# Finishing a stage's two output banks one behind the other, and reading them bank by bank, in a two-block transformer kernel

## The chip, the cores and the metric

The kernel runs on one core of one Trainium2 chip. The metric is the device time of one execution in microseconds (us).

## The reference

`reference()` runs two blocks on 256 tokens of width 1024, all in float32. The first block is a short-convolution mixer and a SwiGLU feed-forward (width 2816), both under adaptive modulation, and a final norm. The second has two layers; each is feed-forward, mixer (a 31-tap convolution with sliding-window attention, or a forgetting attention), feed-forward. What matters here is how a stage ends. In the first block it is `x = x + g * y`; in the second the stage's output `y` is itself normed before it is added:

```
def _rmsnorm(x, g):
    xf = x.astype(jnp.float32)
    y = xf * lax.rsqrt(jnp.mean(xf * xf, axis=-1, keepdims=True) + EPS)
    return (y * g.astype(jnp.float32)).astype(x.dtype)
...
    h = _swiglu(_rmsnorm(x, g[0]), ...)
    x = x + 0.5 * _rmsnorm(h, g[1])
    h = _rmsnorm(x, g[2])
    h = _mixer_even(h, ...)
    x = x + _rmsnorm(h, g[3])
```

## The kernel before

**Eight stages in a row.** CONV, FFN0 (first block), FFN1, AB, FFN2, FFN3, FOX, FFN4 (second block), numbered 0 to 7; `b` is the stage that ends and `s = b + 1` the one that begins. The order of the work on each engine is written out by hand, and semaphores are the only thing that ties the engines together. Tokens are two tiles of 128 (`t` = 0, 1). A weight arrives by DMA (SP's queue) as a unit of 128x2048, is split into a high part by ScalarE (`w_hi`, L995, L1000, L1012) and a low part by VectorE (`w_lo`, L1372, L1377, L1394, L1396), and TensorE forms each product from three matmuls (`product`, L512 to L514).

**How a stage ends.** The output of token tile `t` stands in the two PSUM banks `4+2t` and `5+2t`, 512 columns each. The stage's last weight unit is applied by `down_part` (L557), first for tile 0 and then for tile 1: for each of two contraction slices `k` and each bank `h` one product, so 12 matmuls a tile, and the banks alternate. `y_tok0` counts the end of tile 0 and `w_used` that of tile 1. A few matmuls on a matrix of ones (`keep_warm`, L539) follow.

**What then runs between two stages** (`between`). For the stages of the second block, ScalarE squares all 1024 columns out of PSUM and sums them (`root_y`, L1017, with a read of the accumulator behind it), and takes the root with `eps` as bias (L1019); VectorE takes the reciprocal (L1402), scales the output by it and by a row into `tmp` (`residual`, L1423, 1024 columns), and adds it to `x` in two halves (L1428, 512 columns each, counted by `x_new`). For CONV and FFN0 there is no root of y: VectorE multiplies by a row (L1418) once tile and row are there.

**Order on the engines there.** `s` is NORMED (FFN0, AB, FOX) if its input is normed before it is transposed: VectorE does residual 0, `norm_x` 0 (L1442), residual 1, `turned_lo` 0 (L1453: the low part of the transposed x), `norm_x` 1, `turned_lo` 1. It is FOLDED (FFN1 to FFN4) if x itself is transposed and the norm is folded into later steps: residual 0, `turned_lo` 0, residual 1, `turned_lo` 1. TensorE transposes a tile in two halves of four (`turn_x`, L532; in a FOLDED stage each half waits for its half of x), runs 8 `keep_warm` matmuls, waits for the first `xT_lo` and starts with the first half of tile 0. ScalarE's order in a FOLDED stage is root_y 0, `turned_hi` 0 (L1034), root_y 1, root_x 0, a weight split, `turned_hi` 1; in a NORMED one root_y 0, root_x 0, root_y 1, `turned_hi` 0 and so on. Ahead of all this ScalarE splits the unit `BASE[s] + 1` in four pieces (`split_late`, L1012), and VectorE takes three of these ahead of residual 0 and the fourth behind it.

## Time and profile before

| | us |
|---|---|
| median of 3 runs | 1398.92 |
| lowest and highest run | 1398.75, 1401.97 |
| the profiled execution, its own time | 1401.05 |
| its span, first to last instruction | 1399.3 |
| TensorE (matmuls) busy | 1315.8 (94%) |
| VectorE busy | 831.5 (59%) |
| ScalarE busy | 670.7 (48%) |
| GpSimd busy | 156.8 (11%) |
| DMA queue of the weights, share of 16 engines | 52.9% |

The span is divided into 40 slices on the page, and TensorE is busy nine tenths or more in most of them. Matmuls overlap, so their busy time is above the rate at which they start: 128x512 matmuls last 0.39 us each and start about 0.227 us apart.

### The profile page before, as it was taken

The page shows a single profiled execution, that of the slowest core. Times are in us where ns is not written, and L with a number is a line of the kernel's source. Part 1 is how long each engine was busy: PE and PEld are TensorE (multiplying, and loading weights), DVE is VectorE, ACT ScalarE, POOL GpSimd, SP SyncE. Part 2 cuts the span into 40 slices and gives each one's busy share as a digit, 9 for nine tenths or more (in the row PEclk, how much of TensorE's full clock was granted, in tenths as well). Part 3 has the DMA queues.
Part 4 walks back from the last instruction along what each step waited for, and adds up shares of the span by engine and source line. Part 5 has one row for each costly group of instructions (what it writes and reads, how often), then busy time and mean ns, then how long its engine had stood idle before and what let it go on. Part 6 is the DMA issues. An engine that isn't in the chain of part 4 may idle for free.

```text
span 1399.3 us, 18491 instructions
## 1 busy us (share of the span) xinstructions
PE 1315.8 (94%) x6809; PEld 1101.6 (79%) x6809; DVE 831.5 (59%) x1017; ACT 670.7 (48%) x992; POOL 156.8 (11%) x121
## 2 busy tenths in 40 slices
PE   1869899999899999888999999999999999999998
PEld 1869688888788888776788888888888888788886
DVE  5998665444665555644655556655555477555554
ACT  2304343444554445544654456545544465655443
POOL 1880392000500000200000000000000100000000
PEclk9979999999999999999999999999999999999999
DMA  9967575555355556460375555555572433265551
GB/s 335 343 231 254 181 240 180 182 191 196 106 183 192 194 188 203 142 175 31 122 237 183 180 195 181 180 181 180 184 236 90 150 136 119 93 227 193 180 195 61
DMA packets 171581, 253.64 MB, mean 181 GB/s; under 512 B 9785, under 2 KB 135949, under 8 KB 171533
## 3 DMA queue, kind: packets, MB, share of 16 engines
q1 hardware_dynamic: 168352, 244.33, 52.9%
q0 software_dynamic: 2304, 8.41, 1.6%
q8 instruction: 33, 0.54, 0.2%
q10 hardware_dynamic: 878, 0.25, 0.1%
q14 instruction: 14, 0.11, 0.0%
HBM read 249.77 MB, written 1.05 MB: 179 GB/s over the span
## 4 chain that ended last, share of the span: by engine, by line
PE 84%; DVE 9%; ACT 3%; DMA 1%; issue 1%; POOL 0%; DVEq 0%; SPq 0%; ACTq 0%; POOLq 0%
PE ps L512 26%; PE ps L514 25%; PE ps L513 25%; DVE tmp L1575 2%; PE ps L554 2%; DVE w_lo L1372 2%; DVE x_sb L1428 1%; DMA raw<-in_ada_w 1%; PE ps L813 1%; PE ps L532 1%; DVE tmp L1423 1%; DVE tmp L1525 1%; PE ps L698 1%; ACT w_hi L1012 1%; ACT tmp L1017 0%
## 5 line engine op out<-in xcount | busy, mean ns | idle before, releaser
L512 PE MATMUL ps<-w_lo,xT_hi 128*128 128x512 f32 (+1 forms) x960 | 382.2, 398 | 4.8 <-DVE xT_lo L1453 2.7
L1372 DVE TENSOR_TENSOR w_lo<-raw,w_hi 128x2048 fp32r<-128x2048 f32 x117 | 278.1, 2379 | 166.3 <-ACT w_hi L995 166.3
L514 PE MATMUL ps<-w_hi,xT_lo 128*128 128x512 f32 (+1 forms) x960 | 374.4, 390 | 0.0
L513 PE MATMUL ps<-w_hi,xT_hi 128*128 128x512 f32 (+1 forms) x960 | 374.0, 390 | 0.0
L1377 DVE SCALAR_TENSOR_TENSOR w_lo<-raw,par,w_hi 128x512 fp32r<-128x512 f32 x336 | 230.4, 748 | 139.7 <-ACT w_hi L1000 139.5
L995 ACT ACTIVATE w_hi<-raw 128x2048 fp32r<-128x2048 f32 x117 | 223.5, 1912 | 181.8 <-PE ps L514 160.0
L512 PEld LDWEIGHTS ps<-w_lo,xT_hi 128*128 128x128 f32 x960 | 182.1, 190 | 41.9 <-DVE xT_lo L1453 3.0
L1000 ACT ACTIVATE w_hi<-raw,par 128x512 fp32r<-128x512 f32 x336 | 214.3, 712 | 0.8 <-PE ps L514 0.8
L514 PEld LDWEIGHTS ps<-w_hi,xT_lo 128*128 128x128 f32 x960 | 181.4, 189 | 38.5
L513 PEld LDWEIGHTS ps<-w_hi,xT_hi 128*128 128x128 f32 x960 | 182.2, 190 | 35.6 <-issue 0.2
L512 PE MATMUL ps<-w_lo,hT_hi 128*128 128x512 f32 x400 | 156.5, 391 | 0.0
L514 PE MATMUL ps<-w_hi,hT_lo 128*128 128x512 f32 x400 | 155.7, 389 | 0.0
L513 PE MATMUL ps<-w_hi,hT_hi 128*128 128x512 f32 x400 | 155.6, 389 | 0.0
L512 PE MATMUL ps<-xT_lo,w_hi 128*128 128x256 f32 x360 | 108.7, 302 | 15.9 <-DVE w_lo L1372 13.8
L1092 ACT ACTIVATE hT_hi<-ps 128x512 fp32r<-128x512 f32 x50 | 29.9, 599 | 185.7 <-PE ps L554 185.7
L513 PE MATMUL ps<-xT_hi,w_hi 128*128 128x256 f32 x360 | 105.9, 294 | 0.0
L514 PE MATMUL ps<-xT_hi,w_lo 128*128 128x256 f32 x360 | 105.6, 293 | 0.0
L1499 DVE TENSOR_TENSOR hT_lo<-ps,hT_hi 128x512 fp32r<-128x512 f32 x50 | 34.5, 691 | 103.0 <-ACT hT_hi L1092 103.0
L1087 ACT ACTIVATE act_pair<-ps,stat 128x256 f32<-128x256 f32 x88 | 41.2, 468 | 103.1 <-PE ps L514 103.0
L512 PEld LDWEIGHTS ps<-xT_lo,w_hi 128*128 128x128 f32 x360 | 73.2, 203 | 21.4 <-DVE w_lo L1372 11.2
L513 PEld LDWEIGHTS ps<-w_hi,hT_hi 128*128 128x128 f32 x400 | 75.1, 188 | 15.7 <-issue 0.2
L514 PEld LDWEIGHTS ps<-w_hi,hT_lo 128*128 128x128 f32 x400 | 75.1, 188 | 15.7
(224 smaller groups left out, 1443.5 us busy)
## 6 DMA issues: line engine op xcount, KB each, us to landing
raw<-in_ffn_w_gate SPq DMA_DIRECT2D x88, 512.0 KB, 4.0
raw<-in_ffn_w_up SPq DMA_DIRECT2D x88, 512.0 KB, 4.9
raw<-in_ffn_w_down SPq DMA_DIRECT2D x88, 512.0 KB, 4.1
raw<-in_ffn_w_in SPq DMA_DIRECT2D x44, 512.0 KB, 4.7
raw<-in_conv_w_in SPq DMA_DIRECT2D x24, 512.0 KB, 5.4
raw<-in_fox_w_in SPq DMA_DIRECT2D x24, 512.0 KB, 4.3
raw<-in_ffn_w_out SPq DMA_DIRECT2D x22, 512.0 KB, 4.4
raw<-in_ada_w SPq DMA_DIRECT2D x16, 512.0 KB, 6.5
```

The costliest lines, as they stand in the source:

```text
L512: pe.matmul(o, a_hi, b_lo, start=first, stop=False, skip_group_check=True)
L513: pe.matmul(o, a_hi, b_hi, start=False, stop=False, skip_group_check=True)
L514: return pe.matmul(o, a_lo, b_hi, start=False, stop=last, skip_group_check=True)
L554: tr = pe.transpose(ps[:, 2, f * SEQ + t * P:f * SEQ + (t + 1) * P], hid[:, t, tok(f)], ident[:, :])
L995: act.activation(w_hi[:, slot_of(n), :], raw[:, slot_of(n), :], ACT.Copy).then_inc(hi_ready, 1)
L1000: a = act.activation(w_hi[:, slot_of(n), c], raw[:, slot_of(n), c], ACT.Copy, scale=par[:, g + k:g + k + 1])
L1087: act.activation(sil[:, t, :], ps[:, t, 0:FCH], ACT.Silu, scale=stat[:, 2, c:c + 1] if s in FOLDED else 1.0).then_inc(sil_done, 1)
L1092: act.activation(dst, ps[:, 2, :].rearrange("p (f c) -> p f c", f=2), ACT.Copy).then_inc(hT_hi_ok, 1)
L1372: dve.tensor_tensor(w_lo[:, slot_of(n), :], raw[:, slot_of(n), :], w_hi[:, slot_of(n), :].bitcast(F32), ALU.subtract).then_inc(raw_done, 1)
L1377: o = dve.scalar_tensor_tensor(w_lo[:, slot_of(n), c], raw[:, slot_of(n), c], par[:, g + k:g + k + 1], w_hi[:, slot_of(n), c].bitcast(F32) ...
L1499: dve.tensor_tensor(dst, ps[:, 2, :].rearrange("p (f c) -> p f c", f=2), hi.bitcast(F32), ALU.subtract).then_inc(hT_ok, 1)
L1575: o = dve.scalar_tensor_tensor(acc, ada_v_raw[:, q % 2, i, :], cond[:, k:k + 1], acc, ALU.mult, ALU.add)
```

## The change

The last unit of a stage goes through a new function, `tail_part`, which does both slices of bank `4+2t` and then both of bank `5+2t`, and counts a new semaphore `y_half` after the first bank; the number and the kind of matmuls stay. `root_y` squares and sums each bank by itself, adds `eps` to the first sum with a small activation of its own, and takes the root of the second sum with the first as bias. `residual` does scale, add, scale, add, each on 512 columns, where it did one scale on 1024 and two adds.

```diff
--- before.py
+++ after.py
@@ -283,6 +283,8 @@
         y_tok0 = sem("y_tok0")
         y_sq = sem("y_sq")
         y_std = sem("y_std")
+        y_half = sem("y_half")
+        y_eps = sem("y_eps")
         y_rstd = sem("y_rstd")
         x_sq = sem("x_sq")
         x_std = sem("x_std")
@@ -564,6 +566,18 @@
                                      hi[:, c], lo[:, c], first and k == 0, last and k == 1)
                 return mm
 
+            def tail_part(n, aT_hi, aT_lo, k0, t, ks=(0, 1)):
+
+                hi, lo = unit(n)
+                for h in range(2):
+                    for k in ks:
+                        c = slice(k * D + h * 512, k * D + (h + 1) * 512)
+                        mm = product(ps[:, 4 + 2 * t + h, :], aT_hi[:, k0 + k, tok(t)], aT_lo[:, k0 + k, tok(t)],
+                                     hi[:, c], lo[:, c], False, k == 1)
+                    if h == 0:
+                        mm.then_inc(y_half, 1)
+                return mm
+
             def ffn(s):
                 f, n = ffn_index(s), BASE[s]
                 turn_x(s, 0)
@@ -621,8 +635,8 @@
                 down_part(last - 1, hT_hi, hT_lo, 0, 0, False, False, ks=(1,))
                 down_part(last - 1, hT_hi, hT_lo, 0, 1, False, False).then_inc(w_used, 1)
                 pe.wait_ge(hT_ok, NCH * (f + 1))
-                down_part(last, yT_hi, yT_lo, 0, 0, False, True).then_inc(y_tok0, 1)
-                down_part(last, yT_hi, yT_lo, 0, 1, False, True).then_inc(w_used, 1)
+                tail_part(last, yT_hi, yT_lo, 0, 0).then_inc(y_tok0, 1)
+                tail_part(last, yT_hi, yT_lo, 0, 1).then_inc(w_used, 1)
                 if s != FFN4:
                     keep_warm(WARM_FOLDED if s + 1 in FOLDED and s > FFN0 else WARM_FINAL if s == FFN0 else WARM_NORMED)
 
@@ -754,10 +768,12 @@
             for i in range(4):
                 pe.wait_ge(yT_ok, i // 2 + 1)
                 first, last = i == 0, i == 3
-                mm = down_part(n + 12 + i, yT_hi, yT_lo, 2 * i, 0, first, last)
                 if last:
-                    mm.then_inc(y_tok0, 1)
-                down_part(n + 12 + i, yT_hi, yT_lo, 2 * i, 1, first, last).then_inc(w_used, 1)
+                    tail_part(n + 12 + i, yT_hi, yT_lo, 2 * i, 0).then_inc(y_tok0, 1)
+                    tail_part(n + 12 + i, yT_hi, yT_lo, 2 * i, 1).then_inc(w_used, 1)
+                else:
+                    down_part(n + 12 + i, yT_hi, yT_lo, 2 * i, 0, first, False)
+                    down_part(n + 12 + i, yT_hi, yT_lo, 2 * i, 1, first, False).then_inc(w_used, 1)
                 if i == 2:
                     pe.wait_ge(ada_p_done, ADA_CH)
                     row_everywhere(2, ada_acc)
@@ -864,8 +880,8 @@
             pe.wait_ge(yT_ok, 3)
             down_part(n + 9, yT_hi, yT_lo, 0, 0, False, False)
             down_part(n + 9, yT_hi, yT_lo, 0, 1, False, False).then_inc(w_used, 1)
-            down_part(n + 10, yT_hi, yT_lo, 2, 0, False, True).then_inc(y_tok0, 1)
-            down_part(n + 10, yT_hi, yT_lo, 2, 1, False, True).then_inc(w_used, 1)
+            tail_part(n + 10, yT_hi, yT_lo, 2, 0).then_inc(y_tok0, 1)
+            tail_part(n + 10, yT_hi, yT_lo, 2, 1).then_inc(w_used, 1)
             ffn(FFN2)
             ffn(FFN3)
             n = BASE[FOX]
@@ -944,7 +960,10 @@
 
             def out_part(u, t):
                 pe.wait_ge(oT_ok, 4 + 2 * (u - 12) + 2)
-                mm = down_part(n + u, yT_hi, yT_lo, 2 * (u - 12), t, u == 12, u == 15)
+                if u == 15:
+                    mm = tail_part(n + u, yT_hi, yT_lo, 2 * (u - 12), t)
+                else:
+                    mm = down_part(n + u, yT_hi, yT_lo, 2 * (u - 12), t, u == 12, False)
                 if t == 1:
                     mm.then_inc(w_used, 1)
                 elif u == 15:
@@ -1019,10 +1038,18 @@
                 act.activation(stat[:, 1, c:c + 1], stat[:, 0, c:c + 1], ACT.Sqrt, bias=eps[:, 0:1]).then_inc(std, 1)
 
             def root_y(b, t):
+                e = 2 * (b - FFN1) + t
+                first, second, std = stat[:, 0, STAT_Y + e:STAT_Y + e + 1], stat[:, 2, STAT_Y + e:STAT_Y + e + 1], \
+                    stat[:, 1, STAT_Y + e:STAT_Y + e + 1]
+                act.wait_ge(y_half, 2 * b + t + 1)
+                act.activation(xn[:, t, 0:512], ps[:, 4 + 2 * t, :], ACT.Square, scale=D ** -0.5, accum_out=first).then_inc(y_sq, 1)
+                act.wait_ge(y_sq, 2 * e + 1)
+                act.activation(first, first, ACT.Identity, bias=eps[:, 0:1]).then_inc(y_eps, 1)
                 act.wait_ge(w_used if t else y_tok0, weight_count(y_unit(b)) if t else b + 1)
-                e = 2 * (b - FFN1) + t
-                square_root(STAT_Y + e, ps[:, 4 + 2 * t:6 + 2 * t, :].rearrange("p b n -> p (b n)"), xn[:, t, :],
-                            y_sq, y_std, e + 1)
+                act.activation(xn[:, t, 512:D], ps[:, 5 + 2 * t, :], ACT.Square, scale=D ** -0.5, accum_out=second).then_inc(y_sq, 1)
+                act.wait_ge(y_sq, 2 * e + 2)
+                act.wait_ge(y_eps, e + 1)
+                act.activation(std, second, ACT.Sqrt, bias=first).then_inc(y_std, 1)
 
             def root_x(e, t):
 
@@ -1406,25 +1433,26 @@
             def rms_x(e, t):
                 return reciprocal_root(2 * e + t, x_std, x_rstd, 2 * e + t + 1)
 
-            def output(t):
-                return ps[:, 4 + 2 * t:6 + 2 * t, :].rearrange("p b n -> p (b n)")
-
             def residual(b, t):
 
                 if b == FFN0:
                     dve.wait_ge(ada_row_a, 4)
-                if b <= FFN0:
-                    dve.wait_ge(w_used if t else y_tok0, weight_count(y_unit(b)) if t else b + 1)
-                    dve.tensor_tensor(tmp[:, t, :], output(t), rows[:, 2 if b else 1, :], ALU.mult).then_inc(t_done, 1)
-                    scale = 1.0
-                else:
-                    e = 2 * (b - FFN1) + t
-                    r = reciprocal_root(STAT_Y + e, y_std, y_rstd, e + 1)
-                    dve.scalar_tensor_tensor(tmp[:, t, :], output(t), r, rows[:, 1, :], ALU.mult, ALU.mult).then_inc(t_done, 1)
-                    scale = 1.0 if b in (AB, FOX) else 0.5
-                dve.wait_ge(t_done, 2 * b + t + 1)
+                e = STAT_Y + 2 * (b - FFN1) + t
+                r = reciprocal_root(e, y_std, y_rstd, e - STAT_Y + 1) if b > FFN0 else None
+                scale = 1.0 if b in (CONV, FFN0, AB, FOX) else 0.5
                 for h in range(2):
                     c = slice(h * 512, (h + 1) * 512)
+                    y = ps[:, 4 + 2 * t + h, :]
+                    if b <= FFN0:
+                        if h == 0:
+                            dve.wait_ge(y_half, 2 * b + t + 1)
+                        else:
+                            dve.wait_ge(w_used if t else y_tok0, weight_count(y_unit(b)) if t else b + 1)
+                        o = dve.tensor_tensor(tmp[:, t, c], y, rows[:, 2 if b else 1, c], ALU.mult)
+                    else:
+                        o = dve.scalar_tensor_tensor(tmp[:, t, c], y, r, rows[:, 1, c], ALU.mult, ALU.mult)
+                    o.then_inc(t_done, 1)
+                    dve.wait_ge(t_done, 4 * b + 2 * t + h + 1)
                     o = dve.scalar_tensor_tensor(x[:, t, c], tmp[:, t, c], scale, x[:, t, c], ALU.mult, ALU.add)
                     if b != FFN0:
                         o.then_inc(x_new, 1)
```

**ScalarE from the end of FFN1 into AB** (xn is a scratch output, `stat` a column of sums and roots). Before:

```order
L1017 ACTIVATE xn,stat<-ps 128x1024 [waits y_tok0]
L1019 ACTIVATE stat<-stat,eps 128x1 [waits y_sq]
L1017 ACTIVATE tmp,stat<-x_sb 128x1024 [waits x_new]
L1019 ACTIVATE stat<-stat,eps 128x1 [waits x_sq]
L1017 ACTIVATE xn,stat<-ps 128x1024 [waits w_used]
L1019 ACTIVATE stat<-stat,eps 128x1 [waits y_sq]
```

With the change:

```order
L1045 ACTIVATE xn,stat<-ps 128x512 [waits y_half]
L1047 ACTIVATE stat<-stat,eps 128x1 [waits y_sq]
L1049 ACTIVATE xn,stat<-ps 128x512 [waits y_tok0]
L1052 ACTIVATE stat<-stat 128x1 [waits y_eps,y_sq]
L1036 ACTIVATE tmp,stat<-x_sb 128x1024 [waits x_new]
L1038 ACTIVATE stat<-stat,eps 128x1 [waits x_sq]
L1045 ACTIVATE xn,stat<-ps 128x512 [waits y_half]
L1047 ACTIVATE stat<-stat,eps 128x1 [waits y_sq]
L1049 ACTIVATE xn,stat<-ps 128x512 [waits w_used]
L1052 ACTIVATE stat<-stat 128x1 [waits y_eps,y_sq]
```

Each `root_y` was two activations and is four now; two of the four wait for sums of the engine itself, and both of its squares stand in front of what follows on ScalarE.

**VectorE in the same place, from `norm_x` of tile 0 to `turned_lo` of tile 0.** Before:

```order
L1442 SCALAR_TENSOR_TENSOR xn<-x_sb,stat,rows 128x1024 [waits x_rstd]
L1402 RECIPROCAL stat<-stat 128x1 [waits y_std]
L1423 SCALAR_TENSOR_TENSOR tmp<-ps,stat,rows 128x1024 [waits y_rstd]
L1428 SCALAR_TENSOR_TENSOR x_sb<-tmp,x_sb 128x512 [waits t_done]
L1428 SCALAR_TENSOR_TENSOR x_sb<-tmp,x_sb 128x512
L1453 TENSOR_TENSOR xT_lo<-ps,xT_hi 128x4x128 [waits xT_hi_ok] x2
```

With the change:

```order
L1470 SCALAR_TENSOR_TENSOR xn<-x_sb,stat,rows 128x1024 [waits x_rstd]
L1429 RECIPROCAL stat<-stat 128x1 [waits y_std]
L1453 SCALAR_TENSOR_TENSOR tmp<-ps,stat,rows 128x512 [waits y_rstd]
L1456 SCALAR_TENSOR_TENSOR x_sb<-tmp,x_sb 128x512 [waits t_done]
L1453 SCALAR_TENSOR_TENSOR tmp<-ps,stat,rows 128x512
L1456 SCALAR_TENSOR_TENSOR x_sb<-tmp,x_sb 128x512 [waits t_done]
L1481 TENSOR_TENSOR xT_lo<-ps,xT_hi 128x4x128 [waits xT_hi_ok] x2
```

One instruction on 1024 columns has become two on 512, and the second stands between the two adds; `turned_lo`, for which TensorE waits, is behind all four.

## Rows read from the trace of the kernel before

**Rows 1.** The page: the chain that ended last, share of the span by engine
```profile
PE 84%; DVE 9%; ACT 3%; DMA 1%; issue 1%; POOL 0%; DVEq 0%; SPq 0%; ACTq 0%; POOLq 0%
```
**Rows 2.** Groups by shape: line, engine, out<-in, shape, count | busy us, mean ns
```profile
L1017 ACT ACTIVATE xn<-ps 128x1024 f32<-128x1024 f32 x12 | 12.2, 1018 | 8.5 <-PE ps L514 8.4
L1034 ACT ACTIVATE xT_hi<-ps 128x512 fp32r<-128x512 f32 x28 | 15.7, 592 | 22.0 <-PE ps L532 21.8
L1423 DVE SCALAR_TENSOR_TENSOR tmp<-ps,stat,rows 128x1024 f32<-128x1024 f32 x12 | 15.4, 1284 | 0.4
L1492 DVE SCALAR_TENSOR_TENSOR act_pair<-ps,stat,act_pair 128x256 f32<-128x256 f32 x88 | 39.1, 477 | 16.5 <-ACT act_pair L1087 16.5
L1418 DVE TENSOR_TENSOR tmp<-ps,rows 128x1024 f32<-128x1024 f32 x4 | 4.9, 1214 | 0.0
L1453 DVE TENSOR_TENSOR xT_lo<-ps,xT_hi 128x512 fp32r<-128x512 f32 x28 | 18.2, 685 | 12.6 <-ACT xT_hi L1034 12.1
```
**Rows 3.** Timeline, end of FFN4: start us, us, engine, what [idle before <-releaser]
```profile
1389.72 1.03 ACT L1017 ACTIVATE xn<-ps 128x1024 f32<-128x1024 f32 x1 [6.18 <-PE ps L514]
1390.87 0.29 ACT L1019 ACTIVATE stat<-stat,eps 128x1 f32<-128x1 f32 x1
1391.46 1.28 DVE L1423 SCALAR_TENSOR_TENSOR tmp<-ps,stat,rows 128x1024 f32<-128x1024 f32 x1
1392.78 1.29 DVE L1428 SCALAR_TENSOR_TENSOR x_sb<-tmp,x_sb 128x512 f32<-128x512 f32 x2
```
**Rows 4.** Timeline, CONV to FFN0
```profile
157.03 1.89 DVE L1394 TENSOR_TENSOR w_lo<-raw,w_hi 128x512 fp32r<-128x512 f32 x3 [3.26 <-ACT rows L1185]
158.84 1.22 DVE L1418 TENSOR_TENSOR tmp<-ps,rows 128x1024 f32<-128x1024 f32 x1
174.06 1.09 PE L532 MATMUL ps<-ident,xn 128*128 128x128 f32 x8 [1.95 <-DVE xn L1446]
```
**Rows 5.** Timeline, FFN1 to AB
```profile
552.52 2.20 ACT L1012 ACTIVATE w_hi<-raw 128x512 fp32r<-128x512 f32 x4 [1.68 <-PE ps L514]
555.18 1.03 ACT L1017 ACTIVATE xn<-ps 128x1024 f32<-128x1024 f32 x1 [0.46 <-PE ps L514]
562.01 0.29 ACT L1019 ACTIVATE stat<-stat,eps 128x1 f32<-128x1 f32 x1
562.41 0.16 DVE L1402 RECIPROCAL stat<-stat 128x1 f32<-128x1 f32 x1
565.87 0.50 PE L512 MATMUL ps<-w_lo,xT_hi 128*128 128x512 f32 x1 [1.33 <-DVE xT_lo L1453]
```
**Rows 6.** Timeline, AB to FFN2 (granted clock low at its start)
```profile
671.77 1.28 ACT L983 ACT_TABLE_LOAD   x1
676.90 1.26 PE L532 MATMUL ps<-ident,x_sb 128*128 128x128 f32 x8 [2.37 <-DVE x_sb L1428]
677.99 1.87 PE L539 MATMUL ps<-ones 128*128 128x128 f32 x8
679.51 0.77 PE L512 MATMUL ps<-w_lo,xT_hi 128*128 128x512 f32 x1
681.67 1.29 DVE L1428 SCALAR_TENSOR_TENSOR x_sb<-tmp,x_sb 128x512 f32<-128x512 f32 x2
683.01 1.02 PEld L532 LDWEIGHTS ps<-ident,x_sb 128*128 128x128 f32 x8
```
**Rows 7.** Timeline, FFN2 to FFN3
```profile
863.93 1.03 ACT L1017 ACTIVATE xn<-ps 128x1024 f32<-128x1024 f32 x1
868.76 1.06 PE L539 MATMUL ps<-ones 128*128 128x128 f32 x8
869.74 0.50 PE L512 MATMUL ps<-w_lo,xT_hi 128*128 128x512 f32 x1
872.38 0.39 PE L514 MATMUL ps<-w_hi,xT_lo 128*128 128x512 f32 x1
873.79 0.42 PEld L532 LDWEIGHTS ps<-ident,x_sb 128*128 128x128 f32 x4 [0.18 <-DVE x_sb L1428]
```

## The prediction

> **What bounds the kernel now.** I first read the chain that ended last: 84% of it is TensorE and 12% VectorE and ScalarE [rows 1]. Within a stage TensorE runs without a break, so an edit here is worth something only where TensorE waits, which is between two stages. So I read the timeline of each of the eight stage ends, the idle time ahead of TensorE's instructions above all. Three patterns are to be seen.
>
> First, when a stage ends, VectorE and ScalarE are mostly late for a reason of their own, not because the second bank is missing. Ahead of residual 0 VectorE is still on the weight pieces in CONV, where the scaling starts as they end [rows 4], and FFN0 looks the same. In FFN1 ScalarE's four pieces end at 554.72, and its square of tile 0 starts at 555.18 after only 0.46 us of idle [rows 5]; FFN3 repeats this. In AB a table load ends at 673.05 [rows 6], while tile 0 is complete at about 671.8 (TensorE's work ends 2.37 us ahead of 676.90, and tile 1's twelve matmuls take 2.72 of the time before), and FOX repeats it; in FFN2 the square starts with no idle time before it [rows 7]. Only FFN4 has ScalarE waiting for a long time, 6.18 us [rows 3].
>
> Second, TensorE's restart hangs on whole halves that come late in the order. In a FOLDED stage the second four transposes wait for the second half of x (0.18 us idle in [rows 7]), and the first matmul stands behind them and 8 warming matmuls. In a NORMED one the first matmul waits 1.33 us for `xT_lo`, which stands behind the whole residual of tile 1 [rows 5].
>
> Third, for tile 1 both banks have been complete for microseconds when ScalarE gets to it, so nothing of that tile can start earlier by being read bank by bank.
>
> **What each part costs.** The reordered 12 matmuls cost nothing: same shapes, and runs of twelve on one bank already start 0.227 us apart elsewhere (the first twelve of FFN3 take 2.64 us from first start to last [rows 7], a step of 0.24). Bank one is complete 6 x 0.227 = 1.36 us earlier than bank two; that is all that can be gained on a tile.
>
> *ScalarE's root.* Before: square at 1389.72, root at 1390.87, so 1.15 us [rows 3]. A square of one bank is not shown; the nearest rows are 1018 ns for 1024 columns and 592 ns for 512 [rows 2], so halving takes off 0.42 and square to dependent step is 0.73. The small activation that adds eps is like the root, after which the next instruction can start 0.20 later. With both banks there, root_y takes 0.73 + 0.20 + 0.73 = 1.66 to the root, 0.52 more than before (bounds: 0, if the eps step and the second sum hide behind the first square; 0.61, if the next square starts only when the small one's 0.29 are over). Where bank two is what it waits for, the root comes 0.41 earlier.
>
> *VectorE's residual.* Before: scale 1.284, dependent add 1.32 after its start [rows 3], second add 0.60 after the first, 0.69 long: 2.61. A 512-column scale out of PSUM lies between 477 ns for 256 and 1284 ns for 1024 [rows 2]; the straight line gives 0.746. So 0.79 + 0.60 + 0.79 + 0.69 = 2.87, that is 0.26 more; the first half of x is there after 1.48 instead of 2.01, the second 0.26 later. For CONV and FFN0 it is 1214 against 685 ns [rows 2], 0.19 more a tile. Bounds of the 0.26: 0.05 if a half costs half of 1.284 (0.64), and 0.68 if it costs twice the 477 ns for 256 columns; the line lies between, as VectorE's 685 and 1214 ns do. The Trainium skill (Perfetto Trace Analysis, Optimizing Scalar/DVE Operations) gives a fixed overhead of about 125 ns for a VectorE operation on PSUM and 51 ns for a ScalarE one; with these in place of 0.26 and (with 93 ns for the small one) 0.52, the sum below would be an estimated 2 us, not 6.4. The rows decide, since they hold the semaphore round trips too.
>
> *Stage by stage, in delay of TensorE's stream:*
> - CONV and FFN0: both residuals are on the chain, 2 x 0.19 each: 0.38 + 0.38. The earlier first bank gives nothing, since VectorE is on the weight pieces until then [rows 4].
> - FFN1 and FFN3: the first square can start at 554.62 but the second only after it, so root 0 comes at 556.28 instead of 556.33; x is 0.21 later. Root 1 is queued behind it on ScalarE and 0.52 longer, ready at 562.01 + 0.29 + 0.73 = 563.03, while VectorE was free for it at 562.41 [rows 5]: 0.66. Residual 1 adds 0.26, and `turned_lo` and TensorE's first matmul come 0.92 later: 0.92 + 0.92.
> - AB and FOX: root 0 is 0.52 later, the first half of x comes at the same time, the second 0.78 later, and so do the second transposes, the warming matmuls and the first product [rows 6]. For tile 1 root and scale are 1.30 later and the second half of x 1.56. That half was there at 682.96, and its transposes, the fifth of eight loads from 683.01 on, at about 683.50 [rows 6]; with one 1.56 later and the other 0.78, TensorE waits 0.28 more in AB, and 0.40 in FOX by the same rows there: 1.06 + 1.18.
> - FFN2: ScalarE can take the first square up to 0.2 us earlier, so root 0 is 0.42 late and the second half of x 0.68. For tile 1 there is no slack (TensorE waits for x already, rows 7): another 0.52 + 0.26. Total 1.46.
> - FFN4: root 0 is 0.41 earlier, but the reciprocal of tile 1 then waits for VectorE, which has 0.26 more to do twice: about 0.1 later.
>
> Queued behind the waiting instructions: on ScalarE the weight split of the next stage and `turned_hi` 1, on VectorE the fourth weight piece; both move with the same delay, and their readers on TensorE are as late. SP's weight loads wait for VectorE's low parts and have 47% of the queue's time free. The sum is 0.76 + 1.84 + 2.24 + 1.46 + 0.1 = 6.4 us. Within a stage TensorE has no idle time to absorb it. Against the profiled execution (1401.05, which is 2.1 over the median of the runs shown) this is 1407.5; against the median 1398.9 + 6.4 = 1405.3.
>
> **Rivals.**
> *A, the clock falls at more stage starts (chance 0.17).* After AB, where TensorE has been idle for 2.37 us, the 8 warming matmuls take 1.87 us, and of the twelve behind them the last starts 3.50 us after the first, with the first load of the transposes at 683.01; after FFN2, at full clock, it is 1.06 and 2.64 [rows 6, 7]. A fall costs 0.81 + 0.86 = 1.67 us. FFN1, FFN2 and FFN3 restart at full clock now; their waits grow from 1.33 to some 2.0 us (FFN1, FFN3) and by a new gap of 0.7 in FFN2. If all three fall: 1405.3 + 5.0 = 1410.3. Against it: the gaps stay under AB's.
> *B, ScalarE's additions are hidden (chance 0.17).* If the eps step and second sum cost nothing, only VectorE's part is left: 0.76 for CONV and FFN0, 0.52 each for FFN1 and FFN3, 0.26 each for AB and FOX, 0.5 for FFN2, 0.1: 2.9 us, 1401.8, within what can be told from nothing. For it: root_y's first part has 1.36 us under the second bank wherever ScalarE is free; against it: it is free only in FFN4, and never for tile 1.
> *C, it is faster (chance 0.05).* Mechanism: at tile 0 the root comes 0.41 earlier and the first half of x a further 0.53, and TensorE's transposes start on it. The Trainium skill has the rule for it in the same section as above: breaking up instructions of engines that are not saturated but cause bubbles elsewhere may let work finish sooner. Here it would need ScalarE free when bank one is done, at six stage ends: 6 x 0.94 = 5.6 us, 1393.3. It decides from the point where the square waits for matmuls by over 0.9 us, and only FFN4's does; also TensorE waits for the second half, which comes only 0.15 earlier then.
> *D, the change doesn't do what it says:* covered by the above, since wherever ScalarE is late the two halves are simply one after the other.
>
> **How the numbers follow.** Forecast 0.61, A 0.17, B 0.17, C 0.05. A measurement can tell about 0.3%, 4.2 us, from no change. The forecast of 6.4 us is slower in nearly all of its spread (0.58 of 0.61, with most of its own range from 4 to 9), A is slower (0.17), B the same: slower 0.75, same 0.20, faster 0.05. The range runs from 1401.0, which takes in B, to 1410.5, which takes in A.
>
> **What would show it.** Right: root_y 1 takes about 1.66 us from first square to root; the scales last about 0.75; TensorE's first product after FFN1 is idle for about 2 us before it; FFN2's gap between the two halves of transposes grows to 0.8 or so; TensorE's matmuls in the last unit start 0.227 apart as before. Wrong: if ScalarE's first square starts over 1 us before the second at most stage ends and TensorE's idle times shrink, C holds; if new stretches at 1.2 GHz appear behind FFN1, FFN2 or FFN3, A does.

## The result and the profile after

Nine runs of the changed kernel have a median of 1408.57 us (1403.0 to 1410.38), nine of the kernel before on the same chip 1401.04 (1398.75 to 1402.65). The ratio is 1.0050, 95% interval 1.0036 to 1.0064: **slower by 7.0 us (5.0 to 9.0)**, where 6.4 was forecast. Here and below a difference in us is this ratio's; the medians alone are 7.5 apart. A second series, five runs against nine, gave 1.0055 (1.0041 to 1.0069). The profiled execution took 1407.87 us, its span is 1406.1 (1399.3 before).

The chain of work that ended last, on the page of the changed kernel:

```profile
PE 82%; DVE 10%; ACT 4%; issue 2%; DMA 1%; POOL 0%; SPq 0%; DVEq 0%; ACTq 0%; POOLq 0%
```

TensorE's share fell from 84% [rows 1] by what VectorE and ScalarE gained. TensorE's work is the same (1316.1 us busy against 1315.8). The new instructions in the groups by line and shape (count | busy us, mean ns | idle time before and its releaser):

```profile
L1045 ACT ACTIVATE xn<-ps 128x512 f32<-128x512 f32 x12 | 7.0, 585 | 5.1 <-PE ps L516 5.1
L1047 ACT ACTIVATE stat<-stat,eps 128x1 f32<-128x1 f32 x12 | 3.5, 295 | 0.4
L1049 ACT ACTIVATE xn<-ps 128x512 f32<-128x512 f32 x12 | 7.0, 581 | 0.7 <-PE ps L516 0.7
L1453 DVE SCALAR_TENSOR_TENSOR tmp<-ps,stat,rows 128x512 f32<-128x512 f32 x24 | 17.9, 748 | 0.4
L1451 DVE TENSOR_TENSOR tmp<-ps,rows 128x512 f32<-128x512 f32 x8 | 5.4, 681 | 0.0
```

Both halves together last 1.17 us where the square was 1.018, and 1.50 where the scale was 1.284 [rows 2]. The idle column of the squares tells more: the twelve first squares wait 5.1 us in all, and all of it is FFN4's (4.79 for tile 0 and 0.34 for tile 1). At every other stage end the first bank was there before ScalarE was.

FFN1's end on ScalarE, tile 1 (start, duration, engine, line):

```profile
559.93 0.58 ACT L1045 ACTIVATE xn<-ps 128x512 f32<-128x512 f32 x1
...
560.63 0.29 ACT L1047 ACTIVATE stat<-stat,eps 128x1 f32<-128x1 f32 x1
560.83 0.58 ACT L1049 ACTIVATE xn<-ps 128x512 f32<-128x512 f32 x1
...
561.53 0.29 ACT L1052 ACTIVATE stat<-stat 128x1 f32<-128x1 f32 x1
```

From first square to root it is 1.60 us, one thing behind the other, 1.15 before [rows 3]. VectorE now waits for it, and then does the longer residual:

```profile
561.86 0.16 DVE L1429 RECIPROCAL stat<-stat 128x1 f32<-128x1 f32 x1 [0.32 <-ACT stat L1052]
562.05 0.75 DVE L1453 SCALAR_TENSOR_TENSOR tmp<-ps,stat,rows 128x512 f32<-128x512 f32 x1
562.84 0.69 DVE L1456 SCALAR_TENSOR_TENSOR x_sb<-tmp,x_sb 128x512 f32<-128x512 f32 x1
563.45 0.74 DVE L1453 SCALAR_TENSOR_TENSOR tmp<-ps,stat,rows 128x512 f32<-128x512 f32 x1
564.23 0.69 DVE L1456 SCALAR_TENSOR_TENSOR x_sb<-tmp,x_sb 128x512 f32<-128x512 f32 x1
564.84 1.28 DVE L1481 TENSOR_TENSOR xT_lo<-ps,xT_hi 128x512 fp32r<-128x512 f32 x2
```

And TensorE behind both, at the ends of FFN1 (one row), AB (two) and FFN2 (two, and the last one's weight loads):

```profile
565.58 0.50 PE L514 MATMUL ps<-w_lo,xT_hi 128*128 128x512 f32 x1 [1.99 <-DVE xT_lo L1481]
...
678.96 0.66 PE L534 MATMUL ps<-ident,x_sb 128*128 128x128 f32 x4 [2.31 <-DVE x_sb L1456]
680.35 1.12 PE L534 MATMUL ps<-ident,x_sb 128*128 128x128 f32 x4 [0.73 <-DVE x_sb L1456]
...
872.19 0.66 PE L534 MATMUL ps<-ident,x_sb 128*128 128x128 f32 x4 [0.62 <-DVE x_sb L1456]
...
878.44 0.66 PE L534 MATMUL ps<-ident,x_sb 128*128 128x128 f32 x4 [0.73 <-DVE x_sb L1456]
878.44 0.42 PEld L534 LDWEIGHTS ps<-ident,x_sb 128*128 128x128 f32 x4 [0.97 <-DVE x_sb L1456]
```

The wait for `xT_lo` was 1.33 us before [rows 5]; behind FFN2 the loads of the second half of tile 1's transposes waited 0.18 us [rows 7] and wait 0.97 now. The first half of x does let TensorE start, but TensorE then waits for the second.

Not waiting for the first bank doesn't mean that the early bank had no taker. At FFN1 ScalarE had waited 0.46 us for the second bank in before [rows 5]; now it starts at once, while TensorE is still on that bank. ScalarE's tile 0 and the stage's last matmul, changed and before:

```profile
553.52 0.58 ACT L1045 ACTIVATE xn<-ps 128x512 f32<-128x512 f32 x1
...
555.12 0.29 ACT L1052 ACTIVATE stat<-stat 128x1 f32<-128x1 f32 x1
...
556.37 0.39 PE L516 MATMUL ps<-w_hi,yT_lo 128*128 128x512 f32 x1
```

```profile
556.33 0.29 ACT L1019 ACTIVATE stat<-stat,eps 128x1 f32<-128x1 f32 x1
...
557.48 0.39 PE L514 MATMUL ps<-w_hi,yT_lo 128*128 128x512 f32 x1
```

Against the last matmul the first square is 0.55 us earlier than the one square was (2.85 us ahead of it, where it was 2.30), and the root 0.10 (1.25 ahead, where it was 1.15): the longer chain takes the rest. FFN3 is the same, and in FFN2 the first square is 0.19 earlier and the root 0.26 later.

FFN4 is the only place where ScalarE waits for the first bank:

```profile
1395.17 0.60 ACT L1045 ACTIVATE xn<-ps 128x512 f32<-128x512 f32 x1 [4.79 <-PE ps L516]
...
1396.53 0.60 ACT L1049 ACTIVATE xn<-ps 128x512 f32<-128x512 f32 x1 [0.34 <-PE ps L516]
...
1397.25 0.30 ACT L1052 ACTIVATE stat<-stat 128x1 f32<-128x1 f32 x1
```

From the second square to the root it is 0.72 us, so the root comes 0.43 earlier than with one square.

**One measure for all kernels.** To compare stage ends I took, from the starts of TensorE's rows in the timeline, the time from the last matmul of the ending stage to the thirteenth product matmul of the next (the first of tile 1). It holds all waits of the stage end. "Rest" is everything between these, and the tail is from FFN4's last matmul to the end. In us:

| kernel (profile) | CONV | FFN0 | FFN1 | AB | FFN2 | FFN3 | FOX | sum | tail | rest |
|---|---|---|---|---|---|---|---|---|---|---|
| before | 14.36 | 14.52 | 12.06 | 9.89 | 7.98 | 12.06 | 9.89 | 80.8 | 7.29 | 1311.3 |
| before, 2nd | 14.44 | 13.98 | 12.07 | 9.88 | 7.98 | 12.10 | 9.91 | 80.4 | 7.29 | 1312.5 |
| changed | 14.56 | 14.34 | 12.86 | 11.20 | 9.22 | 12.90 | 11.21 | 86.3 | 7.28 | 1312.5 |
| changed, 2nd | 14.56 | 14.34 | 14.46 | 11.20 | 9.23 | 12.87 | 11.21 | 87.9 | 7.29 | 1311.7 |
| changed, 3rd | 14.54 | 14.69 | 14.44 | 11.20 | 9.23 | 12.87 | 11.81 | 88.8 | 7.28 | 1309.1 |

The stage ends are longer by 5.5 to 8.4 us, 7.1 between the means; the rest is 1311.9 before and 1311.1 changed in the mean, within its scatter. So the whole loss is at the stage ends. Entries of one kernel that differ by 0.3 to 1.6 us (FFN0 14.52 and 14.69, FFN1 14.46 and 14.44, FOX 11.81) are those where the granted clock was at 1.2 GHz in more of that stage end.

The rest's scatter can be accounted for too. Its time at 1.2 GHz is read from the granted clock in the traces: over the fourteen profiles of all kernels here the rest is 1306.4 to 1312.7 us, and less half of its time at 1.2 GHz (34 to 48 us) it is 1288.8 to 1291.3 in all of them.

### The profile page after: what moved, and what is told of

It is laid out like the page before. It is cut to its first block, busy times and chain, and to the rows that moved or that the text cites. A ratio compares the mean times of both kernels' runs of the same rounds, so it can differ in the third digit from the quotient of the medians.

```text
span 1406.1 us, 18555 instructions
## 1 busy us (share of the span) xinstructions
PE 1316.1 (94%) x6809; PEld 1100.2 (78%) x6809; DVE 834.9 (59%) x1033; ACT 675.5 (48%) x1028; POOL 156.7 (11%) x121
## 3 DMA queue, kind: packets, MB, share of 16 engines
HBM read 249.77 MB, written 1.05 MB: 178 GB/s over the span
## 4 chain that ended last, share of the span: by engine, by line
PE 82%; DVE 10%; ACT 4%; issue 2%; DMA 1%; POOL 0%; SPq 0%; DVEq 0%; ACTq 0%; POOLq 0%
PE ps L514 25%; PE ps L516 25%; PE ps L515 25%; DVE tmp L1603 2%; PE ps L556 2%; DVE x_sb L1456 2%; DVE w_lo L1399 2%; DVE tmp L1453 1%; PE ps L829 1%; ACT w_hi L1031 1%; DVE tmp L1553 1%; PE ps L534 1%; DMA raw<-in_ada_w 1%; PE ps L712 1%; ACT tmp L1036 0%
## 5 line engine op out<-in xcount | busy, mean ns | idle before, releaser
L516 PE MATMUL ps<-xT_hi,w_lo 128*128 128x256 f32 x360 | 105.0, 292 | 0.0
```

Of the source, the lines that this page charges most:

```text
L516: return pe.matmul(o, a_lo, b_hi, start=False, stop=last, skip_group_check=True)
```

## Experiments

### e1: the order of the last unit alone

`tail_part` and its semaphore stay, `root_y` and `residual` are those of before.

> Only TensorE's part of the change: the last unit finishes one bank and then the other; root of y and residual read both banks at once as before. The prediction's accounting: 0 us against the kernel before (within its noise of 1 or 2 us), and matmuls 0.227 us apart in the last unit. Rival O, the reordered matmuls themselves cost: the whole loss, +5 to +7 us, shows here.

Measured: 1400.19 us over 12 runs, ratio 0.9998 (0.9989 to 1.0006); stage ends 80.3 us in sum. The order by itself costs and gives nothing, as forecast.

### e2 and e3: ScalarE's part alone, VectorE's part alone

Against e1, e2 adds the new `root_y`, e3 the new `residual`:

```diff
# e2, root_y
-square_root(..., ps[:, 4 + 2 * t:6 + 2 * t, :], ...)
+act.activation(xn[:, t, 0:512], ps[:, 4 + 2 * t, :], ACT.Square, ..., accum_out=first)
+act.activation(first, first, ACT.Identity, bias=eps[:, 0:1])
+act.activation(xn[:, t, 512:D], ps[:, 5 + 2 * t, :], ACT.Square, ..., accum_out=second)
+act.activation(std, second, ACT.Sqrt, bias=first)
# e3, residual, inside the loop over h
+dve.scalar_tensor_tensor(tmp[:, t, c], ps[:, 4 + 2 * t + h, :], r, rows[:, 1, c], ALU.mult, ALU.mult)
```

> TensorE's and ScalarE's part: squares bank by bank, eps step, root; the residual is one scale of 1024 columns and two adds as before. Accounting: root_y 0.52 longer wherever both banks are there; FFN1 and FFN3 +0.4 each, AB +0.5, FOX +0.6, FFN2 +0.9, FFN4 -0.4, CONV and FFN0 0: +2.5 us. Rival B, ScalarE's additions are hidden: 0 or a little below. Rival C, the early square pays: -0.4 to -2.

> TensorE's and VectorE's part: residual scale, add, scale, add on 512 columns; the root of y is one square of 1024 as before. Accounting: 0.26 a residual (0.19 in CONV and FFN0): CONV 0.38, FFN0 0.38, FFN1 and FFN3 0.5 each, AB 0.3, FOX 0.3, FFN2 0.5, FFN4 0.5: +3.4 us. Rival C (the earlier first half of x starts the transposes earlier): 0 or a gain. Rival B puts the whole loss here, as large as in the full change.

Measured: e2 1401.82 us, ratio 1.0011 (1.0003 to 1.0020), +1.5 us; e3 1402.76, ratio 1.0021 (1.0006 to 1.0036), +2.9 us. Expected were 2.5 and 3.4. Their stage ends against e1's:

| | CONV | FFN0 | FFN1 | AB | FFN2 | FFN3 | FOX | tail |
|---|---|---|---|---|---|---|---|---|
| e2 | -0.02 | 0.00 | 0.30 | 0.89 | 0.74 | 0.31 | 1.03 | -0.42 |
| e3 | 0.17 | 0.35 | 0.51 | 0.35 | 0.50 | 0.53 | 0.33 | +0.42 |
| changed | 0.20 | 0.35 | 0.80 | 1.30 | 1.24 | 0.86 | 1.29 | -0.01 |

The third row is the sum of the two above it within 0.08, so the parts are independent, and FFN4's zero is a gain of 0.42 beside a loss of 0.42. The stage ends with the tail say 2.8 and 3.2 us, the ratios of the times 1.5 and 2.9. ScalarE's part is not hidden (rival B), since e2's interval lies above 1, and neither part gains at any stage end between two stages (rival C). Together the ratios give 4.4, not 7.0; where the other 2.6 went is the question of the repeats below.

### e4: without the small step that adds eps

```diff
-act.activation(first, first, ACT.Identity, bias=eps[:, 0:1]).then_inc(y_eps, 1)
```

The kernel leaves out eps in the norm of a stage's output.

> The full change without the small activation that adds eps to the first sum (so the root of y leaves eps out). Accounting: the second square starts 0.20 earlier wherever both banks are there, so some 0.4 less each at FFN1, FFN3 and FFN2, 0.3 each at AB and FOX: 1.9 us less than the change, about +5 against before. If the step is hidden (rival B): as the change, +7.

Measured: 1400.62 us, ratio 1.0008 (0.9996 to 1.0019), 1.1 us where 5 was expected. ScalarE at FFN1's tile 1:

```profile
559.71 0.58 ACT L1045 ACTIVATE xn<-ps 128x512 f32<-128x512 f32 x1
560.19 0.19 ACT L1045 ACTIVATION_READ_ACCUMULATOR xn<-ps 128x1 f32 x1
560.28 0.58 ACT L1047 ACTIVATE xn<-ps 128x512 f32<-128x512 f32 x1
...
560.99 0.30 ACT L1049 ACTIVATE stat<-stat 128x1 f32<-128x1 f32 x1
```

Square to root takes 1.28 us: of the 0.45 that `root_y` became longer, 0.32 is the eps step and its wait, and only 0.13 the second square and sum. FFN1's end is 12.22 us against 12.86, twice 0.32, since both roots stand on its chain; I had counted one. The stage ends are 83.7 us, 2.6 under the changed kernel's first profile (3.2 without FFN0, whose end is 0.6 longer in e4's profile; see e10), where 1.9 was expected. That explains a part of the miss; the rest of the some 6 us between the two ratios (1.0050 and 1.0008) is not at these waits. Between the two profiles the rest differs by another 2.7 us, with 6.9 us less at 1.2 GHz in e4's.

### e5: root 1 directly behind root 0

```diff
                     after(0)
+                    if b > FFN0:
+                        after(1)
                     turned_hi(s, 0)
-                    after(1)
+                    if b == FFN0:
+                        after(1)
                     before(0)
```

and likewise where x is transposed before it is normed.

> The full change, with ScalarE's root_y of tile 1 moved in its queue to directly behind root_y of tile 0 for the stages behind FFN0. My theory (what the change costs is ScalarE's longer root_y of tile 1, which stands in the queue behind turned_hi 0 or root_x 0 and is on the chain to TensorE's first product, plus VectorE's longer residual): the 0.66 us of FFN1 and FFN3 go away, and parts of AB, FOX (0.3 to 0.4 each) and FFN2 (0.8 to 1.4): about 3.4 us less than the changed kernel, so about +3.5 us against the kernel before. Root 1's end should stand ahead of the time VectorE is free for its reciprocal in FFN1 and FFN3, and TensorE's idle time ahead of the first product of the stage behind FFN1 should fall from 1.99 to about 1.4 us. Rival 1 (VectorE alone is the cost): nothing changes, +7 us. Rival 2 (turned_hi 0, now behind a root of 1.6 us, is late and TensorE waits for it instead): +7 us or more.

Measured: 1406.06 us, ratio 1.0042 (1.0028 to 1.0056). FFN1's end on ScalarE, VectorE and TensorE:

```profile
555.20 0.29 ACT L1052 ACTIVATE stat<-stat 128x1 f32<-128x1 f32 x1
```

```profile
559.13 0.15 DVE L1432 RECIPROCAL stat<-stat 128x1 f32<-128x1 f32 x1
```

```profile
562.84 0.50 PE L514 MATMUL ps<-w_lo,xT_hi 128*128 128x512 f32 x1 [1.59 <-DVE xT_lo L1484]
```

Root 1 is done 3.6 us before VectorE takes it, with no wait, and TensorE's wait is 1.59 instead of 1.99, where 1.4 was expected. The stage ends sum to 83.2, 3.1 less than the changed kernel's first profile, against 3.4 expected: FFN1 0.41 (I had said 0.66, but VectorE had waited only 0.32 for root 1), AB 0.63, FFN2 1.20, FOX 0.60. At FFN1 and FFN3 the move gives nothing without the change (e9 against e8, below), so there it is half of the change's price of 0.80. At AB, FFN2 and FOX it also gives 0.73 each without the change, so most of the 0.60 to 1.20 there is a fault of the order, which before has too, and no price of the change. What the change costs in the better order is read from e10 against e9. By its stage ends both rivals fall; by time alone the first would not, as the two ratios' intervals overlap.

### e7, e6, e11, e12: the same kernels again

No edit: the changed kernel twice more (e7 timed, e11), before (e6), and e3 (e12).

> The changed kernel once more, unedited, for a second profile and more times. My theory: of its +7 us, 5.5 to 6 us lie at the seven stage ends (in the first profile 86.3 against 80.8 us over them), and these recur within 0.5 us; the 2.4 us by which AB's inside was longer (107.0 against 104.6) is where stretches at 1.2 GHz happen to fall and does not recur. So the ratio is 1.004 to 1.005. Rival: the 2.4 us in AB recur, and so are caused by the change.

> The kernel before, unedited, for a second profile. If the longer inside of AB (107.0 and 107.1 us in the two profiles of the changed kernel, 104.6 in before) belongs to the change, it is 104.6 again here. If it is only where stretches at 1.2 GHz happen to fall, anything from 104.0 to 107.3 can come, as in the other kernels (e1 106.3, e8 106.2, with AB untouched).

> The changed kernel, unedited, for a third profile. The second had its first twelve matmuls behind FFN1 at 1.2 GHz (stage end 14.46 us), the first did not (12.86). If this is rival A of the prediction in some of the executions, it is 12.9 or 14.5 here, nothing between; the other stage ends recur within 0.1 us.

> The kernel with VectorE's half of the change alone, for a second profile: its times lie in two groups, near 1399 and near 1406 us, at a mean granted clock of 0.982 and 0.976. If the two groups are more or fewer stretches at 1.2 GHz inside the stages, a run near 1406 has the same stage ends (83.0 us in sum, within 0.5, or 1.6 more where a restart falls in one) and is longer inside the stages, with each added stretch visible in the slices of the granted clock. If it is the edit's own waits, its stage ends are longer instead.

Two things came out. **First**, TensorE in the changed kernel's second profile, behind FFN1:

```profile
564.73 0.58 PE L514 MATMUL ps<-w_lo,xT_hi 128*128 128x512 f32 x1 [2.00 <-DVE xT_lo L1481]
565.11 0.63 PE L515 MATMUL ps<-w_hi,xT_hi 128*128 128x512 f32 x1
565.54 0.63 PE L516 MATMUL ps<-w_hi,xT_lo 128*128 128x512 f32 x1
...
568.10 0.55 PE L516 MATMUL ps<-w_hi,xT_lo 128*128 128x512 f32 x1
568.49 0.39 PE L514 MATMUL ps<-w_lo,xT_hi 128*128 128x512 f32 x1
568.72 0.40 PE L515 MATMUL ps<-w_hi,xT_hi 128*128 128x512 f32 x1
```

After the wait of 2.00 us the matmuls start 0.43 apart (1.2 GHz) up to 568.10 and 0.23 apart (2.4 GHz) from 568.49, and the stage end takes 14.46 us instead of 12.86. It is so in two of three profiles of the changed kernel, after waits of 2.00 us; in the one where it was not so the wait was 1.99. None of the other kernels profiled did it, with waits from 1.33 (before) to 1.75 (e2). This is rival A of the prediction, at one of its three places and in some executions; FFN3, with the same wait, did not fall in any of the three.

**Second**, AB's inside took 104.6 us in before and 107.0 in the changed kernel, which looked like a cost of the change. In e7 it came again (107.1), against what I had expected there, and only more profiles told: in the second of before it took 107.3, in the third of the changed kernel 105.0. e7 and e11 missed in a smaller thing too: of the stage ends said to recur, FFN1 (e7), FFN0 and FOX (e11) did not, for their clock. The granted clock by stretch, before and before again (busy time of each engine; the number behind POOL's is TensorE's clock):

```profile
600.00:640.00 40.00, 36.11 (x432) 26.49 (x431) 20.46 (x45) 17.28 (x44) 0.00 (x0) 0.96 0.50 146
640.00:660.00 20.00, 15.29 (x79) 12.09 (x79) 9.59 (x24) 9.34 (x23) 0.00 (x0) 0.83 0.00 1
```

```profile
600.00:640.00 40.00, 36.10 (x420) 25.52 (x420) 21.12 (x45) 16.52 (x42) 0.00 (x0) 0.91 0.46 137
640.00:660.00 20.00, 15.29 (x72) 12.02 (x70) 9.03 (x24) 9.33 (x23) 0.00 (x0) 0.74 0.00 1
```

The same program has more of AB at 1.2 GHz in one execution than in another. And e3 (first) against e12, the same kernel at 1397.1 and 1403.2 us of span (TensorE alone, then its clock):

```profile
600.00:623.00 23.00, 19.11 (x217) 1.00 0.66 191
...
1066.00:1100.00 34.00, 34.00 (x186) 0.95 0.40 124
```

```profile
600.00:623.00 23.00, 19.10 (x173) 0.85 0.65 191
...
1066.00:1100.00 34.00, 33.68 (x158) 0.85 0.30 93
```

The stage ends sum to 83.0 in e3 and 82.8 in e12; the rest is 1306.4 and 1312.7. These 6.3 us lie inside AB (104.0 and 107.0) and FOX (129.9 and 133.2), none at a stage end. By the granted clock each of the two has 6.8 us more at 1.2 GHz in e12, and half of that is 3.4, against 3.0 and 3.3 measured. So these two executions do not differ by the edit's waits, and e3's twelve times fit: the six from 1398.3 to 1400.3 have a mean granted clock of 0.982 or 0.983, the six from 1405.2 to 1407.5 one of 0.974 to 0.979. With such a scatter the times of one edit miss by 2 or 3 us what the stage ends show within 0.1. The stage ends of e2 and e3 add up to 6.0 and the whole change's are 6.0 without FFN1's fall, so the 2.6 us between the ratios are no further cost of the edit: FFN1's fall (1.6 us in two of three profiles, in neither of the parts) is some 1.1 of them in the mean, and scatter the rest. Why the slow stretches fall where they do in an execution stays open.

### e8: the table load ahead

On the kernel before, not the changed one. In AB and FOX ScalarE loads its table for the square root directly ahead of root 0 [rows 6], behind weight pieces before which it idles.

```diff
             split(n + 11)
+            warm_up(ACT.Sqrt)
             split_late(n + 12)
```

and the same in FOX, with `between` loading it for CONV alone.

> The kernel before, with ScalarE's table load for the square root moved ahead in AB and FOX: in before it stands directly ahead of root_y of tile 0 (1.28 us at 671.77), now ahead of the weight split of that place, where ScalarE idles for 2.87 and 2.62 us anyway. My accounting (root 0 is on the chain to TensorE's first product of the next stage in these two): root 0 is 1.28 us earlier, bound by the bank's end at about 671.8, so the two stage ends are 1.2 to 1.3 us shorter each: -2.5 us; if TensorE's shorter wait also keeps it at 2.4 GHz there, up to 1.67 more each, -5.8 us in all. Rival (another wait ends last there, residual or turned_lo): 0.

Measured: 1394.79 us, ratio 0.9964 (0.9950 to 0.9978), 5.0 us faster than before, between the 2.5 and 5.8 of the two cases expected. AB's end on ScalarE and TensorE:

```profile
667.37 2.57 ACT L1012 ACTIVATE w_hi<-raw,par 128x512 fp32r<-128x512 f32 x4 [1.36 <-PE ps L514]
670.03 1.03 ACT L1017 ACTIVATE xn<-ps 128x1024 f32<-128x1024 f32 x1
```

```profile
673.77 1.26 PE L532 MATMUL ps<-ident,x_sb 128*128 128x128 f32 x8 [1.06 <-DVE x_sb L1430]
674.87 1.06 PE L539 MATMUL ps<-ones 128*128 128x128 f32 x8
```

The square follows the pieces at once. TensorE waits 1.06 us instead of 2.37, and restarts at 2.4 GHz: the eight warming matmuls take 1.06 us instead of 1.87 [rows 6]. The two ends are 7.98 us each instead of 9.89: 1.3 each is the shorter wait and 0.6 each what the clock leaves. It leaves that little because tile 1's transposes, which waited for nothing in before, now wait 0.40 us for x. These ends are 3.8 us of the 5.0; the others are unchanged within 0.3.

### e9 and e10: the better order, without and with the change

e9 is e8 with e5's order and FFN4's root bank by bank; e10 is the full change with the same order and table load.

> The kernel before with the table load ahead in AB and FOX (as in e8_table_ahead), root_y of tile 1 directly behind root_y of tile 0 for the stages behind FFN0, and only in FFN4 (the one stage end at which ScalarE waits for the banks) the root bank by bank; residuals whole. By my accounting the early root 1 is worth 0.1 to 0.3 at AB, FOX and FFN2, nothing at FFN1 and FFN3 (VectorE is the later one there without the change), and the bank-by-bank root 0.41 at FFN4: 1.2 us less than e8_table_ahead, about -3.7 us against the kernel before. Rival: as turned_hi 0 is behind a second root, TensorE waits for it: no better than e8_table_ahead.

> The full change (roots and residuals bank by bank at every stage end) put on the better order: the table load ahead in AB and FOX, root_y of tile 1 directly behind root_y of tile 0 behind FFN0. If the price of the change is its extra ScalarE and VectorE time on the chain, whatever the order, the stage ends are longer than those of e9_combined by: CONV 0.2, FFN0 0.35, FFN1 0.4, AB 0.8, FFN2 0.8, FFN3 0.4, FOX 0.8, FFN4 0.4: +4.1 us against e9_combined (about 1397 us, ratio to before 0.998). Rival (breaking the instructions up pays once ScalarE is free for the first bank): no slower than e9_combined, 1393 us.

Measured: e9 1393.0 us, ratio 0.9957 (0.9944 to 0.9971), **6.0 us faster than before, and 15 under the changed kernel's median of the same series (1408.25)**. The early root 1 is worth 0.73 at each of AB, FFN2 and FOX (against e8), not the 0.1 to 0.3 expected, and nothing at FFN1 and FFN3, as expected. e10 1395.87, ratio 0.9963 (0.9950 to 0.9977). The stage ends and the tail:

| | CONV | FFN0 | FFN1 | AB | FFN2 | FFN3 | FOX | tail |
|---|---|---|---|---|---|---|---|---|
| e9 | 14.35 | 13.97 | 12.04 | 7.25 | 7.25 | 12.07 | 7.25 | 6.87 |
| e10 | 14.55 | 14.94 | 12.45 | 8.01 | 8.02 | 12.46 | 8.01 | 7.28 |

Column by column e10 is 0.2 to 0.97 longer, 4.7 us in sum, against 4.1 expected. FFN0's 0.97 is the miss; e5 had 0.36 there with the same code, and e4 the same 14.94. In e4 and e10 TensorE's granted clock fell to 1.2 GHz 5.3 and 5.4 us behind the stage's last product, in e5 6.6 us behind it, in e9 not within that end. That this makes the other 0.6 is likely, but not shown. The intervals of the two ratios overlap, so by time alone the rival is not excluded; by the stage ends it is. It is a fair test of the rival, since in e10 the early bank of tile 1 does have a taker. ScalarE and VectorE at FFN1's end:

```profile
556.05 0.60 ACT L1049 ACTIVATE xn<-ps 128x512 f32<-128x512 f32 x1 [0.34 <-PE ps L516]
...
556.77 0.29 ACT L1052 ACTIVATE stat<-stat 128x1 f32<-128x1 f32 x1
```

```profile
560.71 0.15 DVE L1434 RECIPROCAL stat<-stat 128x1 f32<-128x1 f32 x1
```

Tile 1's second square waits 0.34 us for its bank, so the first ran under it, and root 1 stands 0.42 earlier against the stage's last matmul than in e9. VectorE takes it 3.7 us after its end, and the stage end is 0.41 longer all the same. Even with ScalarE free earlier, reading bank by bank costs at every stage end but FFN4's for the root. In e9, where only FFN4 has the split root, its tail is 0.42 shorter: that is the one piece of the change worth keeping.

## Why the prediction was right

- **Where the change acts.** It said that ScalarE is mostly late for reasons of its own, so that the earlier bank gives next to nothing outside FFN4: 0.05 at FFN1. The idle column of L1045 shows that ScalarE waits for a first bank in FFN4 alone; at FFN1 the root is 0.10 earlier, at AB and FOX later. That the new order costs nothing is e1's.
- **ScalarE's 0.52** was 0.45 (1.60 us and not 1.66): square to dependent step takes 0.70, not 0.73, and stands in it twice. The 0.41 at FFN4 was 0.43. Two sums go 0.04 past their own figures: 563.03 less 562.41 is 0.62 and not 0.66, and in AB 682.96 + 1.56 is 0.24 behind 683.50 + 0.78 and not 0.28. VectorE's own lateness of 0.21 is within the 0.62, so it would have waited 0.4 for root 1; its wait was 0.32.
- **VectorE's 0.26** was right: 562.05 to 564.92 is 2.87 us, and the interpolated 0.746 for a scale is 748 ns. e3's FFN2, with two residuals on the chain, has 0.50.
- **By stage end**, forecast against measured (means of the profiles; FFN0 against e1, FFN1 and FOX without the profiles whose clock fell there): CONV 0.38, 0.15; FFN0 0.38, 0.35; FFN1 0.92, 0.80 without the clock; AB 1.06, 1.31; FFN2 1.46, 1.25; FFN3 0.92, 0.80; FOX 1.18, 1.31; FFN4 0.1, 0.0. The sum is 6.0 for 6.4. FFN1 and FFN3 are shorter by ScalarE's 0.07 and by a root 0 that is 0.10 and not 0.05 earlier. In FFN2 root 0 is 0.26 late and not 0.42, and root 1 has 0.45 for 0.52. Two more terms were mis-sized. In CONV the residuals added 0.58 (tile 1's first add lasted 0.89 us, not 0.69), but 0.39 was taken back by the `xn` row of tile 1 behind them, in before and in the changed kernel:

```profile
169.87 2.08 DVE L1442 SCALAR_TENSOR_TENSOR xn<-x_sb,stat,rows 128x1024 f32<-128x1024 f32 x1
```

```profile
169.78 1.69 DVE L1470 SCALAR_TENSOR_TENSOR xn<-x_sb,stat,rows 128x1024 f32<-128x1024 f32 x1
```

In AB and FOX the first product came 1.19 and 1.05 later, not 0.78: the second half's transposes, which ran ahead of the clock's fall in before (the eight to their warming matmuls 1.09, [rows 6]), now run behind it, 0.90 for four (680.35 to 681.25). Tile 1 then added 0.12 and 0.27 and not 0.28 and 0.40.
- **How near the number came** owes something to luck: the terms above are 0.8 too high at six ends and 0.4 too low at two, and the clock's fall behind FFN1, which the sum did not hold, added 1.1 in the mean. The absolute 1405.3 was 3.3 under the median of 1408.57; 2.1 of that is the base, since nine runs of before have their median at 1401.04 and the three that it was added to had it at 1398.92.
- **Rival A** (0.17) came in part: one fall of three (behind FFN1, never behind FFN2 or FFN3), in two of three profiles, at 1.60 us for the 1.67 forecast. With it the mean over profiles is 7.1, and the times say +7.0. **Rival B**: e2 and e4 exclude it; in the changed kernel the eps step costs 0.32 a root and hides nowhere but in FFN4. **Rival C**: its condition, a square that waits for matmuls by over 0.9 us, held at FFN4 alone, where the root came 0.43 earlier and VectorE's longer residuals took 0.42 back.
- **The rule of the Trainium skill** (Perfetto Trace Analysis, Optimizing Scalar/DVE Operations), that breaking up instructions may let work finish sooner, held for the root in FFN4 (e2's tail 0.42 shorter), and for the whole change at no stage end. The same section's overheads of about 125 and 51 ns would have given an estimated 2 us; the stage ends measured 5.5 or more; what a piece costs here is the step that depends on it (0.32 for the eps step, e4) more than its own start (0.13).

## What to carry to other kernels

Splitting an instruction so that it can start on half its input pays only where its engine stands idle for longer than the split adds (here 0.45 us for the root and 0.26 for the residual), and where the engine behind it is waiting for the result: at FFN1 a first square 0.55 us earlier gave a root 0.10 earlier, and e10's early root 1 gave nothing. Read the idle time before that very instruction, and before its reader, at every place. If it is zero, look at what stands ahead of it in its queue: a table load moved into idle time gave 5 us, where the split lost 7. A loss or gain of a few us is read from the stage ends of one or two profiles, and a second profile of the same kernel tells which differences belong to the edit.

## What was not expected of the hardware

- One kernel's times span 9 us (e3, 1398.3 to 1407.5 in 12 runs), and two profiled executions of it 6.1 us with the same stage ends (83.0 and 82.8), through how much of AB and FOX runs at 1.2 GHz. Half of the time at 1.2 GHz, taken off, leaves 1288.8 to 1291.3 us outside the stage ends in all fourteen profiles.
- The same wait of 2.0 us behind FFN1 was followed by 1.2 GHz in two executions and by 2.4 GHz in a third; behind FFN3 it was followed by 2.4 GHz in all three. After 1.06 us (e8, AB) TensorE came back at 2.4 GHz, after 2.31 us (AB, changed) at 1.2, and after only 1.83 us (AB, e3 and e12) at 1.2 too. So the length of the wait alone does not decide; what does stays open.
- A square with a sum is followed on ScalarE by a read of the accumulator, 0.19 us as a row of its own, but with no dependent step between them the next square starts 0.57 after the first (e4), so the read hides; the eps step adds 0.32.
